# Local attention: the gate products dealt anew between the jobs, and the reciprocal put between two maxima

## The reference, cut to what matters

```python
def window_gqa(q, k, v, q_c, k_c, v_c, sink, with_ctx):
    group = A_HEADS // A_KV_HEADS            # 8 query heads on 2 key heads, 64 wide
    scale = A_HD ** -0.5
    ...
    def block(n, qg):                        # one block of 128 queries
        start = n * BLK
        k_win = lax.dynamic_slice_in_dim(k_pad, start, span, axis=1)
        ...
        valid = ((jnp.abs(pos_k[None, :] - pos_q[:, None]) <= A_WINDOW)
                 & (pos_k[None, :] >= 0) & (pos_k[None, :] < n_tok))
        p_win, p_ctx = joint_softmax([jnp.where(valid, score(qg, k_win), -jnp.inf), score(qg, k_c)], sink_f)
        return values(p_win, v_win) + values(p_ctx, v_c)
```

## Time and profile before

| | us |
|---|---|
| median of 3 runs | 3203.41 |
| the profiled execution | 3200.36 |
| span of its trace | 3198.5 |
| TensorE busy | 3101.4 (97%) |
| VectorE busy | 1697.0 (53%) |
| ScalarE busy | 1157.5 (36%) |
| GpSimd busy | 229.6 (7%) |
| local attention in layer 0 | 427 to 581 |
| local attention in layer 1 | 2160 to 2275 |

### The profile page before, as it was taken

How to read it: one execution, slowest core, us unless ns; L and a number is a source line. 1 busy time by engine, 2 the same in 40 slices (tenths; PEclk the granted TensorE clock), 3 DMA queues, 4 the chain that set the end, 5 groups by cost and what they waited for, 6 DMA issues and landing times. The chain is left out here.

```text
span 3198.5 us, 46148 instructions
## 1 busy us (share of the span) xinstructions
PE 3101.4 (97%) x18246; PEld 2787.4 (87%) x18246; DVE 1697.0 (53%) x3086; ACT 1157.5 (36%) x1961; POOL 229.6 (7%) x184
## 2 busy tenths in 40 slices
PE   8999999999999999999999999999999999899999
PEld 6999978998899889999999988877787887888887
DVE  5655366433366866763222575547544578664334
ACT  4233344333313554222212442435443236442223
POOL 1001000100020020000000010110100210100000
PEclk9999999999999999999999999999999999999999
DMA  8312411320241124531222453141321521443333
GB/s 286 123 40 67 125 54 27 121 65 27 79 165 53 41 80 139 165 114 55 75 66 59 148 164 96 57 142 38 108 66 40 179 79 40 145 145 98 106 88 103
DMA packets 353231, 309.32 MB, mean 97 GB/s; under 512 B 40638, under 2 KB 329356, under 8 KB 351756
## 3 DMA queue, kind: packets, MB, share of 16 engines
q1 hardware_dynamic: 331022, 240.65, 25.2%
q10 hardware_dynamic: 22014, 65.99, 5.6%
HBM read 272.89 MB, written 33.29 MB: 96 GB/s over the span
## 5 line engine op out<-in xcount | busy, mean ns | idle before, releaser
L1068 PE MATMUL ps<-u_hi,w_hi 128*128 128x384 f32 (+1 forms) x2040 | 588.5, 350 | 4.4 <-issue 3.0
L1068 PE MATMUL ps<-u_hi,w_lo 128*128 128x384 f32 (+1 forms) x2040 | 582.5, 347 | 0.0
L1068 PE MATMUL ps<-u_lo,w_hi 128*128 128x384 f32 (+1 forms) x2040 | 582.4, 347 | 0.0
L2298 DVE TENSOR_TENSOR w_lo<-w_raw,w_hi 128x2048 fp32r<-128x2048 f32 x129 | 298.8, 2316 | 349.9 <-ACT w_hi L1722 347.4
L1068 PEld LDWEIGHTS ps<-u_hi,w_hi 128*128 128x128 f32 x2040 | 369.0, 188 | 26.8 <-issue 7.2
L1068 PEld LDWEIGHTS ps<-u_hi,w_lo 128*128 128x128 f32 x2040 | 372.4, 188 | 18.7
L1068 PEld LDWEIGHTS ps<-u_lo,w_hi 128*128 128x128 f32 x2040 | 372.4, 188 | 17.9
L1427 PE MATMUL ps<-u_hi,w_hi 128*128 128x384 f32 (+1 forms) x816 | 305.6, 375 | 9.7 <-ACT space L2086 7.6
L1722 ACT ACTIVATE w_hi<-w_raw 128x2048 fp32r<-128x2048 f32 x129 | 246.1, 1908 | 150.3 <-issue 69.4
L1427 PE MATMUL ps<-u_hi,w_lo 128*128 128x384 f32 (+1 forms) x816 | 296.5, 363 | 0.2
L1427 PE MATMUL ps<-u_lo,w_hi 128*128 128x384 f32 (+1 forms) x816 | 295.5, 362 | 0.0
(11 more groups left out here) (317 smaller groups left out, 5272.6 us busy)
## 6 DMA issues: line engine op xcount, KB each, us to landing
w_raw<-in_w_in SPq DMA_DIRECT2D x288, 256.0 KB, 3.8
w_raw<-in_w_gate_up SPq DMA_DIRECT2D x176, 256.0 KB, 4.0
space<-in_w_mod SPq DMA_DIRECT2D x40, 1024.0 KB, 5.3
w_raw<-in_w_down SPq DMA_DIRECT2D x114, 192.0 KB, 2.9
w_raw<-in_w_branch SPq DMA_DIRECT2D x64, 256.0 KB, 3.6
w_raw<-in_w_out SPq DMA_DIRECT2D x48, 256.0 KB, 3.8
m_scratch<-space ACTq DMA_DIRECT2D x3, 3072.0 KB, 10.0
space<-m_scratch ACTq DMA_DIRECT2D x3, 3072.0 KB, 10.2
```

The lines of the kernel that those rows point to most:

```text
L1068: last = nc.tensor.matmul(ps[:, 2 * (t % 2) + b, 0:a1 - a0], wv[w][:, k, j * P:(j + 1) * P], xx[:, k, a0:a1], start=(k == 0 and w == 0 and ...
L2298: V.tensor_tensor(w_lo[slot][:, :], w_raw[slot][:, :], w_hi[slot][:, :].bitcast(F32), ALU.subtract).then_inc(w_lo_done, 1)
```

## The change

Three things are changed, all in "attend a". The quotas: in layer 0 every odd job has 4 gate products and every even job 8, from job 18 on 12; in layer 1 odd jobs have 4 (twice 2) and even jobs 6, 7 or 9. The number of products ahead of `value_pair` in an even job is now a list, `AHEAD_A`: 4 in layer 0, 3 (twice 2) in layer 1, where it was all but two of the quota. The tails take 24 and 14 products in place of 16 and 11. And on VectorE `denominators(i)` stands in odd jobs between the maxima of i + 1 and of i + 2, where it was behind both; latent attention ("c"), which shares that code, gets the same order.

```diff
     QUOTA = {
-        "a": ([12] + FOUR + THREE + [6, 12, 6] + 2 * THREE + [12, 6, 6] + THREE + [6, 6, 12] + 2 * THREE + [6, 12, 6] +
-              2 * THREE + [9, 5, 5, 5] + [4, 4],
-              [12] + [5, 5, 5, 5, 4] + [5, 5, 5, 9] + [5, 5, 5, 5, 4] + [5, 5, 9, 5] + FOUR + [4, 4, 8, 4, 4] +
-              [5, 4, 4]),
+        "a": ([12] + 8 * [4, 8] + 15 * [4, 12], [12] + 2 * [4, 6, 4, 6, 2, 9, 4, 6, 4, 7, 4, 6, 4, 6] + [4, 6]),
...
+    AHEAD_A = ([6] + 23 * [4], [6] + 2 * [3, 3, 2, 3, 3, 3, 3] + [3])
     HEAD = {"a": (12, 12), "c": (0, 0), "d": (20, 20)}
-    TAIL = {"a": ((3, 4, 9), (2, 3, 6)), "c": ((8, 8, 16), (8, 6, 18)), "d": ((8, 36, 12), (8, 17, 7))}
+    TAIL = {"a": ((4, 8, 12), (3, 4, 7)), "c": ((8, 8, 16), (8, 6, 18)), "d": ((8, 36, 12), (8, 17, 7))}
...
                 def before(i):
-                    return max(plan.quota[i] // 2, plan.quota[i] - 2) if kind == "a" else plan.quota[i] // 2
+                    return plan.AHEAD_A[l == DEPTH - 1][i // 2] if kind == "a" else plan.quota[i] // 2
...
                     else:
-                        for j in range(i + 1, min(i + 3, len(jobs)) if i % 2 else 0):
+                        later = range(i + 1, min(i + 3, len(jobs)) if i % 2 else 0)
+                        for j in later[:1]:
                             maxes(j)
                         denominators(i)
+                        for j in later[1:]:
+                            maxes(j)
```

## The result

| | before | after |
|---|---|---|
| median, us | 3203.41 | 3218.77 (5 runs, 3216.35 to 3219.35) |
| the profiled execution | 3200.36 | 3219.35 |
| span of its trace | 3198.5 | 3217.5 |
| TensorE busy | 3101.4 | 3102.4 |

The ratio after to before is 1.005, with an interval of 1.004 to 1.0061: slower, by 15.4 us of the medians. TensorE's busy time is the same; what grew is the time in which it stands. In the profile after, the lines of `attend` carry numbers lower by 2 (L1523 is now L1521, L2086 is L2084, L2874 is L2872).

The account below looks back on a forecast made before the run. TensorE was taken as the bound: 33.5 us of new stalls replace 17.2, +16.3 us, giving 3216.7 us from the profiled execution or 3219.7 from the median. 3218 us was taken, range 3210 to 3226.

Parts of the forecast that it names:

- The floor: Earliest start of value products, set by VectorE's copy: 4.11 us after the scores (four key tiles), 4.65 (five), unmoved.
- The new stalls: TensorE standing before value products in the pairs of jobs: 19.7 us in layer 0, 13.2 us in layer 1.
- the context pairs: Layer 0 pairs of two key tiles: TensorE stands 0.3 to 0.5 us; seven counted at 0.3.
- The overlap: TensorE's 23 waits before the change: 0.25 us lost beyond idle in each, 18.0 us in all, 17.2 to be won.
- Evictions: Nine chunk ends covered only by value products: 0 to 0.25 us of waiting each, 0.6 us taken in all.
- The third rival: TensorE's clock falls in both stages: a tenth of 269 us is 27 us, giving 3245 us; chance 0.04.
- A hole between the maxima: On VectorE, idle time there would fit the reciprocal for nothing: 25 us less, 3193 us; chance 0.05.
- The first, ScalarE's half alone: Only ScalarE's copy half holds the value products: floors 0.4 to 0.5 us lower, 15 us less, 3203 us; chance 0.05.
- The fourth: Evictions still hold TensorE at nine chunk ends inside pairs: 7 us, not 0.6; 3224 us; included in the forecast's 0.86.
- a held maximum: VectorE's maximum behind the reciprocal might wait for the emptied pipe: 38 pairs x 0.08 would add 3 us.

Follow-up runs that it names:

- the exchange alone: Kernel before with only the reciprocal moved between the two maxima in odd jobs, quotas of gate products unchanged: 3200.86 us, ratio 0.9996.
- VectorE's copy moved forward: Kernel after with VectorE's half of the odd job's probabilities copy ahead of the second maximum, ScalarE's half unmoved: 3204.92 us, ratio 1.0008.
- the last kernel: Kernel after with both halves of the odd job's copy first, nine inside evictions ahead of the second exponential, token tile rounded at odd job's start: 3187.03 us, ratio 0.9947.
- the new dealing alone: Kernel after with the reciprocal put back behind both maxima, new dealing of gate products kept: 3218.81 us, ratio 1.0047.
- the kernel after again: Kernel after, unchanged, measured once more as common measure for a later group of runs: 3216.54 us, ratio 1.0042.
- the old dealing with both copies first: Kernel before with its own quotas, reciprocal between the maxima and both halves of the odd job's copy first: 3212.41 us, ratio 1.0031.
- both copies first: Kernel after with VectorE's copy half ahead of the second maximum, ScalarE's ahead of the next exponential, token tiles rounded last: 3202.52 us, ratio 1.0001.
- the eviction kernel: Kernel after with both copy halves first and, in nine even jobs where a chunk ends inside, eviction ahead of the second exponential: 3191.74 us, ratio 0.9966.

## Why the prediction was right

Forecast 3218 us, measured 3218.77. The mechanism is the one forecast. That the two agree within 1 us is partly luck: 3218 was taken between 3216.7 and 3219.7, by the base of the profiled execution or of the median, and the loss itself, forecast at 16.3 us, was measured at 15.4 and then at 13.4.

- *The floor.* Rightly taken as the end of VectorE's chain, which the exchange leaves in its place (behind six other instructions in both orders, where the prediction says seven): the copy 2.57 us after the first maximum for 2.63, the value products at 4.65 us (five tiles, layer 0) and 4.11 (four), as read from the earlier trace rows. It is shown from two sides, by the exchange alone (the same end of the wait under another name) and by VectorE's copy moved forward (the floor falls to 4.21).
- *The new stalls.* Predicted 0.90 us for five tiles, 0.80 for four, 0.3 in the context pairs; measured 0.86, 0.74 and 0.20 to 0.38 of idle time, to which some 0.07 comes for the overlap that is lost: 520.12 follows the transpose of 518.99 by 1.13 us, where 0.20 is usual (508.74 to 508.94 in the last kernel), so 0.93 lost with 0.86 shown. In layer 1 0.61 to 0.64 and 0.53 for 0.67 and 0.57. Over a layer: 18.2 + 22 x 0.07 = 19.7 us for the 19.7 predicted; 11.3 + 15 x 0.07 = 12.4 for 13.2.
- *The overlap.* The 0.25 us per wait was read from a gate product that waits for an eviction and used for all 23 waits of the kernel before. The transposed reciprocal loses nearly as much: with the new dealing alone the value products come 0.92 us later than where nothing waits (4.65 for 3.73), with 0.69 shown. Value products that wait for the copy lose 0.07. Four of the 23 are of that kind, priced 0.7 us too high together: 16.5 us were to be won by this estimate, and the best kernel gained 15.6.
- *Evictions.* Predicted 0.6 us, measured none beyond the first. In the kernel after they had cover only because the value products stood: with VectorE's copy moved forward they are back, 6.3 us with the first.
- *The stages.* From the second scores to the first product of the next phase, layer 0 took 152.97 us before and takes 165.57 now (427.63 to 593.20), layer 1 110.19 and 114.96 (2179.57 to 2294.53). Their ends, before and after in turn:

```profile
580.65 0.41 PE L1068 MATMUL ps<-y_hi,w_hi 128*128 128x384 f32 x1 [0.26 <-issue]
2274.81 0.47 PE L1068 MATMUL ps<-y_hi,w_hi 128*128 128x512 f32 x1 [0.26 <-issue]
```

```profile
593.20 0.41 PE L1066 MATMUL ps<-y_hi,w_hi 128*128 128x384 f32 x1 [0.26 <-issue]
2294.53 0.47 PE L1066 MATMUL ps<-y_hi,w_hi 128*128 128x512 f32 x1 [0.26 <-issue]
```

  That is +12.6 and +4.8 us, 17.4 for the 16.3 predicted. In the kernel after again the stages take 164.03 us (427.66 to 591.69) and 114.89 (2177.97 to 2292.86): +11.1 and +4.7, 15.8 in all, where the prediction's terms give 11.7 and 4.6. The 1.5 us between the two executions of the same kernel are the clock (next point). The profiled executions of before and after differ by 19.0 us; the other 1.6 lie outside the two stages. There the granted clock falls three times before (in the windows 1800 to 1810, 1890 to 1900 and 2610 to 2620) and four times after (from 1020, 1480, 1810 and 1900 on), each time by some 1.7 us of work, and one fall more would be the 1.6.
- *The third rival, in small.* In the first pair of layer 0 the profiled execution lost its clock for some 4 us:

```profile
428.00:430.00 2.00, 1.38 (x9) 0.95 (x6) 1.53 (x5) 2.00 (x5) 0.00 (x0) 0.88 0.00 0
430.00:432.00 2.00, 2.00 (x8) 1.56 (x7) 1.56 (x5) 1.53 (x8) 0.00 (x0) 0.50 0.00 0
432.00:434.00 2.00, 2.00 (x15) 1.65 (x14) 0.74 (x3) 0.00 (x0) 0.00 (x0) 0.77 0.00 0
```

  The pair takes 6.5 us for 5.0 before. The change didn't cause it: the kernel after again has no such fall, with the same waits in the same place (0.71, 0.20 and 0.62 us), and the exchange alone and the fastest kernel have it. The 37 new waits, up to 1.6 us long and one in each pair but the first, cost no clock in either execution of this kernel. That the clock can fall in these stages, which the rival feared, is shown by the old dealing with both copies first.
- *The other rivals.* A hole between the maxima doesn't exist: the add and the reciprocal push the second maximum back by their own length (1.64 us behind the first for 0.99). The first, ScalarE's half alone, is refuted by VectorE's copy moved forward. The fourth has no eviction wait to show.

The failures were in the expectations of the later kernels. For both copies first and for the eviction kernel the sum left out the token tiles, which the last kernel shows to cost some 5 us. For the old dealing with both copies first it left out what stands behind the copy on ScalarE, and the clock.

## What to carry to other kernels

A wait names only what ended last. Ask what stands behind that instruction in its own queue before moving it: the reciprocal was moved 0.99 us forward, and the copy behind it kept TensorE to the same instant. Work that covers a chain must be as long as the chain in every pair, so shorten the chain first (here by putting what TensorE needs next ahead of what it needs a microsecond later) and deal the cover afterwards. And an instruction put first delays all that it passes: copy, eviction and token tile each had to get their place before 15 us came of it; the copies alone had brought nothing, or a loss of 9.

## What the runs showed of the hardware

- The clock can fall after one long wait, and doesn't after each. In the old dealing with both copies first TensorE stood seven times for 1.71 to 2.21 us, and behind six of these waits the granted clock went down to 0.50 to 0.53 in a stretch of 2 us, at a cost of some 1.7 us of work each; the full clock stayed behind one of 1.92 us. Shorter waits mostly cost nothing of it: the 37 of up to 1.6 us in the kernel after, in two executions, and one of 1.69 us with both copies first. But in the kernel with VectorE's copy first it fell behind waits of 0.21, 0.28 and 0.98 us within 3 us (2183.26 to 2185.95; then 0.57 and 0.57 in two stretches of 2 us), and the three short waits at the start of layer 0 (0.71, 0.20 and 0.62 us) cost some 1.7 us in three of the thirteen profiled executions and nothing in the others. The Trainium skill (TensorE: Matmul & The Clock Gate, A second HAM failure mode: psum-queue depth-cycling) has a kernel whose clock swings by frequent short idles between groups of matmuls. Here the clock swings in the old dealing with both copies first, at some 10 us in 330, but behind few and long waits; the kernel after, with the more frequent and shorter ones, doesn't show it.
- What a wait costs TensorE beyond its idle time goes by the instruction held: 0.25 us for a gate product behind transposes, 0.23 for a transpose and value products held by the reciprocal, 0.07 for value products held behind their transpose.
- Two Vector instructions can overlap a little: the maximum behind the reciprocal starts at 518.72, and the reciprocal ends at 518.80. The Trainium skill (VectorE: DVE Perf Modes, The DRAIN you can't avoid) has a Vector instruction wait for the emptied pipe of the last, and lets one that isn't held start earlier; the trace agrees with the second half. The 3 us that the prediction put on a held maximum did not come: the copy begins 2.57 us behind the first maximum, for 2.63 before.
